# Layer norms in token layout: seeded sums, no residual matmuls, and one weight unit split on GpSimd in each norm

## The reference

```python
def _layer_norm(x, g, b):          # per token, over the 1024 features
    return (x - mean(x)) * rsqrt(var(x) + LN_EPS) * g + b

# first block, layer l = 0, 1
mix = einsum(merged, w_out[l])     # merged: three attention branches, gated
x = _layer_norm(ALPHA * x + mix, ln1_g[l], ln1_b[l])
ffn = einsum(silu(u_gate) * u_up, w_ffn_out[l])
x = _layer_norm(ALPHA * x + ffn, ln2_g[l], ln2_b[l])

# second block, layer l = 0, 1
x = layer_norm(ALPHA * x + 0.5 * swiglu(x, ...ffn1...), ln1_g[l], ln1_b[l])
mix = concatenate([y_a, y_b, y_c]) @ w_out[l]      # conv, gmlp, sparse attention
x = layer_norm(ALPHA * x + mix, ln2_g[l], ln2_b[l])
x = layer_norm(ALPHA * x + 0.5 * swiglu(x, ...ffn2...), ln3_g[l], ln3_b[l])
```

## Time and profile before

| | us |
|---|---|
| runs | 2028.13, 2027.08, 2028.14; median 2028.13 |
| profiled execution: span | 2026.5 |
| PE busy | 2010.1 (99%), 14176 matmuls |
| DVE busy | 1274.6 (63%) |
| ACT busy | 927.4 (46%) |
| POOL busy | 32.2 (2%) |
| DMA | 352.5 MB, mean 174 GB/s |

### The profile page before, as it was taken

The page is one execution under the profiler, slowest core; times in us unless marked ns, Lnnn a source line. Parts: engine busy times, 40 slices in busy tenths (PEclk is TensorE's granted clock), DMA queues, the critical chain, the costliest instruction groups (busy, mean ns, idle before and its releaser), DMA issues.

```text
span 2026.5 us, 32504 instructions
## 1 busy us (share of the span) xinstructions
PE 2010.1 (99%) x14176; PEld 1838.1 (91%) x14176; DVE 1274.6 (63%) x1844; ACT 927.4 (46%) x1275; POOL 32.2 (2%) x56
## 2 busy tenths in 40 slices
PE   8999999999999999999999999999999999999998
PEld 7888999999887999999999989799999998979997
DVE  6566666555756665655665567765566556776555
ACT  4445444443545444544444454454444445445442
POOL 0000000000000000000000000000000000000000
PEclk9999999999999999999999999999999999999999
DMA  8543555666554556496556646458656664545663
GB/s 287 167 151 132 187 169 170 196 207 190 167 163 138 166 167 186 144 266 187 167 177 189 189 134 167 103 158 252 187 167 187 188 188 133 160 135 158 188 190 101
DMA packets 416133, 352.51 MB, mean 174 GB/s; under 512 B 28816, under 2 KB 361080, under 8 KB 415992
## 3 DMA queue, kind: packets, MB, share of 16 engines
q1 hardware_dynamic: 415992, 350.44, 57.3%
HBM read 349.36 MB, written 1.05 MB: 173 GB/s over the span
## 4 chain that ended last, share of the span: by engine, by line
PE 94%; DVE 3%; ACT 2%; issue 0%; DMA 0%; DVEq 0%; SPq 0%
PE ps L201 29%; PE ps L203 29%; PE ps L202 29%; PE ps L1446 2%; PE ps L1527 2%; PE ps L1565 1%; DVE hl L1990 1%; PE ps L1599 1%; ACT hl L1749 1%; DVE er L2157 0%; DVE small L2116 0%; ACT er L1841 0%; PE ps L1637 0%; DVE er L2114 0%; PE ps L1570 0%
## 5 line engine op out<-in xcount | busy, mean ns | idle before, releaser
L1990 DVE TENSOR_TENSOR hl<-raw,hl 128x1024 fp32r<-128x1024 f32 (+2 forms) x555 | 756.3, 1393 | 393.4 <-ACT hl L1749 392.4
L201 PE MATMUL ps<-xt,hl 128*128 128x256 f32 (+1 forms) x2672 | 753.9, 282 | 0.0
L202 PE MATMUL ps<-xt,hl 128*128 128x256 f32 (+1 forms) x2672 | 746.2, 279 | 0.0
L203 PE MATMUL ps<-xt,hl 128*128 128x256 f32 (+1 forms) x2672 | 745.9, 279 | 0.0
L1749 ACT ACTIVATE hl<-raw 128x2048 fp32r<-128x2048 f32 (+1 forms) x323 | 613.2, 1900 | 182.8 <-PE ps L203 169.5
L201 PEld LDWEIGHTS ps<-xt,hl 128*128 128x128 f32 (+1 forms) x2672 | 501.0, 187 | 4.6 <-issue 1.5
L202 PEld LDWEIGHTS ps<-xt,hl 128*128 128x128 f32 (+1 forms) x2672 | 501.1, 188 | 3.1
L203 PEld LDWEIGHTS ps<-xt,hl 128*128 128x128 f32 (+1 forms) x2672 | 500.8, 187 | 0.2
L201 PE MATMUL ps<-hl,o 128*128 128x512 f32 x656 | 261.5, 399 | 0.0
L203 PE MATMUL ps<-hl,o 128*128 128x512 f32 x656 | 259.0, 395 | 0.0
L202 PE MATMUL ps<-hl,o 128*128 128x512 f32 x656 | 258.8, 394 | 0.0
(11 more groups left out here) (202 smaller groups left out, 1606.5 us busy)
## 6 DMA issues: line engine op xcount, KB each, us to landing
raw<-in_w_in SPq DMA_DIRECT2D x83, 1024.0 KB, 5.1
raw<-in_w_ffn_in SPq DMA_DIRECT2D x88, 512.0 KB, 5.1
raw<-in_ffn_gate SPq DMA_DIRECT2D x88, 512.0 KB, 4.1
raw<-in_ffn_up SPq DMA_DIRECT2D x88, 512.0 KB, 5.3
raw<-in_ffn_down SPq DMA_DIRECT2D x44, 1024.0 KB, 5.1
raw<-in_w_ffn_out SPq DMA_DIRECT2D x22, 1024.0 KB, 5.0
raw<-in_w_out SPq DMA_DIRECT2D x12, 1024.0 KB, 5.1
raw<-in_w_branch_a SPq DMA_DIRECT2D x8, 1024.0 KB, 4.9
```

Source lines behind the costliest of these rows:

```text
L201: e.matmul(out, l[0], r[0], start=start, stop=False)
L202: e.matmul(out, l[0], r[1], start=False, stop=False)
L203: return e.matmul(out, l[1], r[0], start=False, stop=stop)
L1990: e.tensor_tensor(lo[:, c], m["raw"][:, k % NRAW, 0:n][:, c], hi[:, c].bitcast(F), ALU.subtract).then_inc(s.low.up(("low", k), *([("low", ...
```

## The change

**Residual.** The step `residual`, `ai` and all 320 of its matmuls are gone. ACT copies x from `X` into the PSUM bank before the first product (`seed`, 128x512, four per norm), and all products are added onto it (`mm3_onto`, never with a start flag). This needs banks whose every column was last written by a matmul, so rings know `dense` banks, and start and stop flags of other matmuls are set once per bank.

**Norm.** Gain and bias go on in token layout, as in the old last norm: `ln_norm` is now four DVE passes of 128x512 per half, and X holds the norm's result. `ln_turn` transposes it, and `ln_split` splits straight from PSUM: ACT two copies of 128x512, DVE four subtractions of 128x256. The two residual steps behind the last piece of i = 1, and those between A and B, are gone; in front of an ffn the second transposition now stands in the middle of B's first pass.

**Rows.** `rows_in` brings g and b, spread over 128 partitions, as four DMAs of 128x512 (1 MB in all) for each norm, into four free ring buffers. SP waits for the buffers and until the norm before has read its rows. They are taken during the ffn or the merge before; for norms 6 and 9, right behind norms 5 and 8.

**Low halves.** B's two low halves in a norm are done by POOL (`pool_low`) instead of DVE.

```diff
+def mm3_onto(e, out, l, r):
+    e.matmul(out, l[0], r[0], start=False, stop=True, skip_group_check=True)
+    e.matmul(out, l[0], r[1], start=False, stop=True, skip_group_check=True)
+    return e.matmul(out, l[1], r[0], start=False, stop=True, skip_group_check=True)
...
-    def in_halves(pieces, more=None):
+    def in_halves(pieces):
...
         pieces(0, 0, (0, 1))
-        if more:
-            more()
-            turn()
-            pieces(1, 0, (0, 1))
-        else:
-            pieces(1, 0, (0,))
-            turn()
-            pieces(1, 0, (1,))
-        affine()
+        pieces(1, 0, (0,))
+        turn()
+        pieces(1, 0, (1,))
+        split()
...
         turn(0)
         tail[3]()
-        rest()
-        affine(0, lambda: low(2))
+        for _ in range(2):
+            low(2, "pool_low")
+        split(0)
         stats(1)
-        low(2)
...
-        for j, b in enumerate(first_units([gate_up(0), gate_up(1)], begin)):
+        for j, b in enumerate(first_units([gate_up(0), gate_up(1)])):
             up(j, b, True)
+        acc = [acc_pair(i=0)]
         up(2)
+        acc.append(acc_pair(i=1))
         up(3)
+        rows_in(g, b_, row_slots())
...
-        layer_norm(acc, cols[:, 12:28], cols_event, tail)
+        layer_norm(acc, tail)
+        rows_in(I["ln2_g_2"][l], I["ln2_b_2"][l], [RT.take() for _ in range(2)] + [Place(m["sg"][:, 1, c * 512:(c + 1) * 512], ("merge split", 1)) for c in range(2)])
...
+    def rows_in(srcs, places, v):
+        for src, x in zip(srcs, places):
+            e.wait_ge(*T[x.before])
+        e.wait_ge(*T["rows read", v - 1] if v > 1 else (None, 0))
+        for src, x in zip(srcs, places):
+            e.dma_start(x.ap, src.partition_broadcast(128)).then_inc(s.rows.up(("rows", v)), 16)
...
+    def ln_split(i, banks, v):
+        for q, b in enumerate(banks):
+            e.wait_ge(*T[b.full])
+            e.activation(XT[:, 0, 4 * q:4 * q + 4, i * 128:(i + 1) * 128], b.ap.rearrange("p (k t) -> p k t", k=4), ACT.Copy).then_inc(
+                done.up(("xt high", v, i, q)), 1)
+    def seed(b, i, c, x_event):
+        e.wait_ge(*T[x_event])
+        e.wait_ge(*T[b.before])
+        e.activation(b.ap, X[:, i, c * 512:(c + 1) * 512], ACT.Copy).then_inc(done.up(b.seed), 1)
...
+    def pool_low(k, n, h, parts):
+        hi, lo = P.m["hl"][:, k % NHL, 0, 0:n], P.m["hl"][:, k % NHL, 1, 0:n]
+        c = slice(h * n // parts, (h + 1) * n // parts)
+        e.wait_ge(*T["high", k])
+        e.tensor_tensor(lo[:, c], P.m["raw"][:, k % NRAW, 0:n][:, c], hi[:, c].bitcast(F), ALU.subtract).then_inc(
+            s.pool_low.up(("low", k), ("low", k, h)), 1)
...
+    def ln_norm(i, acc, small, rows, v, out="xn"):
+        mv, rs = small[1:3]
+        e.wait_ge(*T["rows", v])
+        e.wait_ge(*T["x turned", v - 1, i])
+        e.wait_ge(*T["mv", v, i])
         for c in range(2):
+            e.scalar_tensor_tensor(X[:, i, c * 512:(c + 1) * 512], acc[c].ap, mv[:, 0:1], rows[c].ap, ALU.subtract, ALU.mult).then_inc(done.up(acc[c].free), 1)
         e.wait_ge(*T["rs", v, i])
         e.wait_ge(*done.now)
         for c in range(2):
             x = X[:, i, c * 512:(c + 1) * 512]
+            e.scalar_tensor_tensor(x, x, rs, rows[2 + c].ap, ALU.mult, ALU.add).then_inc(
+                done.up((out, v, i, c), *([("rows read", v)] + [r.free for r in rows if r.ring] if i and c else [])), 1)
```

More of the change, by code:

```diff
@@ L178, in __init__, with take @@
         self.order, self.latest = list(range(len(aps))), [None] * len(aps)
-    def take(self):
-        slot = self.order.pop(0)
+        self.dense, self.spare = [False] * len(aps), None
+    def take(self, dense=None):
+        dense = self.spare if dense is None else dense
+        like = [x for x in self.order if dense is None or self.dense[x] == dense]
+        slot = like[0] if like or dense else self.order[0]
+        self.order.remove(slot)
         self.n += 1
@@ L520, in proj_t, with first_units @@
         return t_unit(*t_proj(*args, **kw))
-    def first_units(two, more):
+    def first_units(two):
         P.ahead = 1
@@ L525, in first_units, with rows_in, row_slots, layer_norm @@
         us = [P.unit(segs, UNIT) for segs in two]
[L526 removed]
+        bs = dense([PB.take() for _ in two])
         def pieces(n, i, parts):
             for p in [q for p in parts for q in (2 * p, 2 * p + 1)]:
[L530 to L536 removed]
+                add("first_piece", us[n], bs[n], i, p, xt_i(v, i, p), p == 0 and i == 0, p == 3 and i == 1)
+        in_halves(pieces)
+        return bs
+    def rows_in(g, b, places):
+        P.rows = places
+        add("rows_in", [x[c * 512:(c + 1) * 512] for x in (g, b) for c in range(2)], places, P.xv + 1)
+    def row_slots():
+        return [ET.take() for _ in range(4)]
+    def layer_norm(acc, tail, final=False):
         v = P.xv
[L539 to L541 removed]
+        rows, P.rows = P.rows, None
         P.xv += 1
@@ L576, in layer_norm, with seed, acc_pair @@
         tail[3]()
-        rest()
-        affine(0, lambda: low(2))
+        for _ in range(2):
+            low(2, "pool_low")
+        split(0)
         stats(1)
-        low(2)
-        P.half = (lambda: turn(1), lambda: affine(1))
-    def residual(acc, c):
-        v = P.xv
-        add("residual", acc[0][c], 0, c, xt_events(v), True, [("xt read", v, 0)] if c else [])
-        yield 0.9
+        for x in rows:
+            if x.ring is ET:
+                ET.give(x)
+            elif x.ring is RT:
+                RT.give(x)
+        P.half = (lambda: turn(1), lambda: split(1))
+    def seed(b, i, c):
+        dense([b])
+        add("seed", b, i, c, ("xn", P.xv, i, c) if P.xv else ("x", i))
+    def acc_pair(i=None, c=None):
+        pair = [PB.take(True), PB.take(True)]
+        for n, b in enumerate(pair):
+            seed(b, *((i, n) if c is None else (n, c)))
+        return pair
     def out_part(w, acc, src_events, c, r=0, ks=(0, 2)):
@@ L1018, in swiglu @@
         f = ("second", l, which)
-        return ffn(f, gate_up, I[f"ffn{which}_down_2"][l], 0.5, before, setup)
+        n = 1 if which == 1 else 3
+        return ffn(f, gate_up, I[f"ffn{which}_down_2"][l], 0.5, before, (I[f"ln{n}_g_2"][l], I[f"ln{n}_b_2"][l]), setup)
     def second_setup(l, o):
@@ L1293, in lin_out @@
                     P.flush()
-                for i in range(2):
-                    acc[i].append(PB.take())
-                yield from residual(acc, c)
+                for i, b in enumerate(acc_pair(c=c)):
+                    acc[i].append(b)
+                PB.spare = None if c else False
                 yield from out_part(I["w_out_2"][l], acc, [[("o1 gmlp", l)], [("o1 conv", l)]], c, ks=(2, 0))
@@ L1517, in ln_turn, with out_piece @@
             turn(b, [X[:, i, (4 * q + k) * 128:(4 * q + k + 1) * 128] for k in range(4)], ("x turned", v, i))
-    def residual(b, i, c, events, first, after):
-        if first:
-            e.wait_ge(*T[b.before])
-        e.wait_ge(*T["ai"])
-        for x in events:
-            e.wait_ge(*T[x])
-        for k in range(4):
-            for z in (0, 1):
-                ins = e.matmul(b.ap[:, k * 128:(k + 1) * 128], XT[:, z, 4 * c + k, i * 128:(i + 1) * 128], ai, start=first and k == 0 and z == 0,
-                               stop=not first and k == 3 and z == 1)
-        ins.then_inc(done.up(b.full, *after), 1)
-    def out_piece(g, b, r, i, ks, src_events, last, events):
+    def out_piece(g, b, r, i, ks, src_events, events):
         hi, lo = (x.rearrange("p (k c) -> p k c", k=4) for x in hl(g, UNIT))
```

241 lines of the change are left out of this document (85 added, 156 removed).

## The result

The changed kernel takes 2030.81 us (median of 18 runs), the kernel before beside it 2027.95 us: the ratio is 1.0016, with a 95% interval of 1.0009 to 1.0023. The predicted time was 2010. The profiled execution has a span of 2029.1 us, 2.6 more than before. Some 35 us of TensorE work are gone, and some 37 us of waiting and slow running have come in their place.

What follows compares the result with a forecast made beforehand. PE was taken as the bound. Terms -34.7 - 0.8 + 6.6 + 10.0 + 0 + 1.0 = -17.9 us on a span of 2026.5, plus 1.7 to the median, gave 2010; range 2000 to 2028, 8 in 10 and a little more.

Steps and rivals of the forecast that it cites:

- PE was the bound: Whole kernel: PE, busy for 99% of the span, sets the time as the sum of its matmuls from start to start.
- whatever goes from PE counts in full: Residual steps: 320 matmuls of 0.108 us removed from PE, none beside other work, gain 34.7 us.
- The norm's own chain: Norms: PE waits for DVE's normalization passes, 0.85 us in five norms and 0.6 in four, +6.6 us.
- the old 0.8: Norms 2, 5 and 8: PE's old waits of 0.27 us for XT of i = 1 go, gain 0.8 us.
- POOL's halves: B's low halves in the norms: each below 2.4 us on POOL, which costs nothing.
- the bound by the small rows: POOL's low half in the norms: upper estimate 4.3 us, from 3.5 times DVE's 1.22 us.
- C's load: Behind norms 5 and 8: load held on SP behind the rows, PE waits 5.0 us twice, +10.0 us (7.2 to 12.6).
- The seeds and the attention: ACT's seeds: 0 ahead of D's high half; in sparse attention an assumed 0.5 us twice, +1.0 us (0 to 3).
- Engines shut each other out: Rival, norms: POOL's SBUF reads keep DVE's passes waiting, up to 2.4 us per norm, 2032 us; chance 0.05.
- The change doesn't do what it says: Rival: each norm's chain takes the dropped matmuls' place, 3.5 us per norm, 2028 us; chance 0.05.
- the worst end of the sum: Whole kernel: every term at its worst gives +2.9 us, 2031 us.
- the seeds in front of an ffn: Six norms: two seeds ahead of D's high half on ACT, counted 0, bound 7.2 us.

Runs made afterwards that it cites:

- e11: The kernel before with half of each residual step left out (low part of x missing, 160 of 320 matmuls gone): 2018.82 us, ratio 0.9958.
- e8: e3 with an extra POOL subtraction of 128x512 ahead of B's first low half in each norm: 2021.45 us, 13.2 us slower than e3.
- e1: The changed kernel with the rows for norms 6 and 9 asked for later on SP, so C's load is ahead of them: 2012.54 us, ratio 0.9926.
- e2: The changed kernel with the first w_out seed in the sparse attention put earlier on ACT, ahead of the last pair's exponentials: 2026.61 us.
- e3: The changed kernel with both edits of e1 and e2: 2008.21 us, 4.3 us less than e1.
- e6: e1 with the planner given back the residual step's 0.9 us behind the w_out seeds in the attention: 2008.85 us.
- e5: e3 with the planner given back the residual step's 0.9 us behind the w_out seeds in the attention: 2008.88 us.
- e9: e3 with the low halves of units in the attention's second half (8 a layer) done by POOL instead of DVE: 2022.46 us.
- e10: e3 with the attention's low halves done by POOL instead of DVE only from the last convolution unit on: 2014.58 us.
- e12: The kernel before with only the GpSimd part of the change, B's two low halves in each norm on POOL: 2047.04 us, ratio 1.0098.
- e7: The changed kernel with 44 unused transpositions on PE behind units A and B of norms 5 and 8: 2027.28 us, ratio 1.0000.

## Why the prediction was wrong, point by point

- **PE was the bound, its time the sum of its matmuls: right. That whatever goes from PE counts in full: wrong.** The matmuls are gone as counted (319 of them, from start to start, make 34.9 us in the old trace; 320 x 0.108 is 34.6 and not the 34.7 of the prediction, which changes nothing). But in e11 half of them brought 9.2 us, not 17.3. The sentence "all on PE, none beside other work" looked at PE's idle time and not at how late the other engines were.
- **The norm's own chain, +6.6 us less the old 0.8: right.** In the seven norms without C the table gives 26.0 - 21.7 = 4.3 us for the waits, net, where 4 x 0.6 + 3 x 0.85 - 0.27 = 4.7 were worked out. The waits stand where they were put, and are shorter: the five norms behind an ffn wait 0.23 us at the first transposition, where I had 0.5, and not at the second, where I had 0.3; the four behind `w_out` wait 0.27 to 0.30 at the second, where I had 0.6. That is 2.3 us in all, and what is missing to 4.3 lies in gaps too small to be listed.
- **POOL's halves: right.** 2.40 us each (18 of them, 2388 to 2415 ns), at the limit that was worked out; the power of i = 1 starts right behind them (1190.93 after 1186.21 + 4.76), and e8 shows that there is no slack. The estimate by the Trainium skill ("GPSIMD Engine Reference", Elementwise) was 2.25, near the measured 2.40; the bound by the small rows, 4.3, was far off.
- **C's load, +10.0 us: mechanism right, size wrong.** Measured by e1: 18.3, beyond the bound of 12.6. Of this the wait is 6.2 and 7.0 us instead of 5.0 (C's high half began 7.8 and 8.5 us after the issue, where the range ended at 7.8), and 2.1 and 1.6 us are the clock. "I take 5.0" chose the middle of a range that had the rows ahead of C in it and left out D's load close behind.
- **The clock: not in the sum.** The prediction has no word on it. A wait of 4 to 7 us on PE costs about 2 us more behind it, here four times, an estimated 7.4 us in all. Without it the changed kernel would by that estimate be some 4 us faster than the one before.
- **The seeds and the attention, +1.0 us: the step that failed.** I looked at where ACT's two seeds stand ahead of D's high half, and there they cost nothing, as said. For the attention I assumed 0.5 us per layer without reading its timeline. Measured against what its residual matmuls should have brought (-1.7 us a layer): +5.8 and +5.3 us in the table, so 7.5 and 7.0 us more, 14.5 in all, the clock's 2 us each among them. Two things came together: the seed sits on ACT behind the exponentials, and the planner moved `w_out` forward once the step's 0.9 us were out of its count. The term was assumed, with a bound of 3 us, and not worked out from a chain. e2, e3 and e6 show that either edit takes back 4 us. About 10 of the 14.5 us are left in e3. That they are ACT's and DVE's own chains is read from the waits, which move and stay in e5; no run shows it by shortening these chains, since e9 and e10 put POOL in DVE's way.
- **The rivals.** "Engines shut each other out" did not come in the changed kernel, but e12 and e9 show that the mechanism is there and what it costs; it was missed by the place alone: POOL starts at 1698.45 while DVE's last pass over two SBUF inputs runs until 1698.58. Its time of 2032 is near the measured 2031 by chance. So is that of "The change doesn't do what it says", 2028: the norms' chains didn't take the matmuls' place. And so is the worst end of the sum, 2031: the terms for C and the attention went beyond their bounds (18.3 for 12.6, 14.5 for 3), while those for the norms and the seeds in front of an ffn stayed far within theirs.

The sum as measured: 2028.0 - 0.4 - 34.9 (residual) + 5.0 (all norms' waits, net of the old ones) + 18.3 (C, by e1) + 14.5 (attention) = 2030.5, against 2030.8.

The best version that came of it, e3, takes 2008.2 us, 1.0% less than the kernel before. That this is near the 2010 that the prediction had for the change as it stood is chance: e3 is without C's wait, which is in the 2010, and with 10 us in the attention, which are not.

What stays open: how much of the 7.8 and 8.5 us of C's load is due to the rows ahead of it and how much to D's load behind it, and how much of the attention's remaining loss a better order could take back; e5 and e6 restored the old order only, and the clock blurs what it is worth.

## What to carry to other kernels

Before work is taken off the bounding engine, read at each place how late the next engine is, by taking half of it out if need be; a step that goes from a plan also takes its share of the planner's time with it. A load that is put ahead on a queue with a wait for the present stage holds back all that stands behind it: ask where in the queue it could wait without anyone behind. And price a wait on TensorE of some microseconds with the slow clock that follows it.

## What the runs showed of the hardware

- TensorE's granted clock fell to 0.50 (1.2 GHz) in or behind the four waits of 4.1 to 7.0 us of the changed kernel, and the matmuls behind ran slowly for 3.4 to 4.8 us, 213 ns for one of 256 columns instead of 117. It fell as well at waits of 2.98 us (e6), 2.36 (e7) and 2.00 (e5).
- At shorter waits it was not the same each time. Behind 1.45 us it fell both times in e12, and behind 1.66 us in two of four places of e8. Behind two waits of 1.50 and 1.15 us close together it fell in layer 1 of e2 (0.64 on average from 1294 to 1296) and not in layer 2, in e3 the other way round, and in e8 in both. Behind single waits of 1.2 us (e12, and e7 behind norm 5), of 1.04 us (e11) and of 0.6 us (the kernel before) it stayed at 1.00.
- A DVE subtraction with both inputs in SBUF (128x256, 0.42 us) took up to 2.60 us beside a POOL subtraction (128x1024, 2.40 us), and a multiplication of 128x512 (0.69 us) up to 2.87 in e9; with one input in PSUM it took 0.42 beside the same.
- POOL's subtraction of 128x1024 took 2.40 us where DVE's takes 1.22, twice as long; that of 128x512 took 1.29 us (e8). The ratio of the two small instructions of 128x1 (POOL's power 0.54 us, DVE's addition 0.15), 3.5, said nothing about it.
